# RWKV chunk loop on one core: token copies and two transposed inverses made two heads per product, heads laid out by parity of the pair

## What is computed

```python
def _wkv7_scan(r, decay, k, v, kk, a):          # 16 heads of 64
    def step(state, inp):
        r_t, w_t, k_t, v_t, kk_t, a_t = inp
        sk = jnp.einsum('bhij,bhj->bhi', state, kk_t)
        state = (state * w_t[:, :, None, :]
                 - sk[..., None] * (kk_t * a_t)[:, :, None, :]
                 + v_t[..., None] * k_t[:, :, None, :])
        y = jnp.einsum('bhij,bhj->bhi', state, r_t)
        return state, y
```

## Time and profile before

| what | value |
|---|---|
| median of 3 runs | 2909.34 us (2909.28 to 2913.61) |
| the profiled execution | 2909.81 us, its span 2907.8 us |
| busy in the span | PE 2583.3 us (89%), DVE 1611.4 (55%), POOL 1259.4 (43%), ACT 941.8 (32%) |
| first instruction of the recurrent stage on VectorE with data | 1628.8 us |
| first and last state update begin | 1700.6 and 2067.3 us |

### The profile page before, as it was taken

The page is one execution under the profiler, slowest core; times in us unless marked ns, Lnnn a source line. Parts: engine busy times, 40 slices in busy tenths (PEclk is TensorE's granted clock), DMA queues, the critical chain, the costliest instruction groups (busy, mean ns, idle before and its releaser), DMA issues. The chain is left out here.

```text
span 2907.8 us, 52077 instructions
## 1 busy us (share of the span) xinstructions
PE 2583.3 (89%) x21600; PEld 2089.2 (72%) x21600; DVE 1611.4 (55%) x1957; ACT 941.8 (32%) x1535; POOL 1259.4 (43%) x630
## 2 busy tenths in 40 slices
PE   2887888999999999989999577777799999999999
PEld 2565667788887788767777466666687888788887
DVE  7744455655543633376865489888335333434334
ACT  3435433322223222244544333333333222122221
POOL 3522334444445444444334345454355444444443
PEclk9889999999999999999999799989899999999999
DMA  7511224354442232237666544443332323232223
GB/s 254 186 61 38 87 88 152 130 181 160 168 144 89 86 106 96 94 98 188 156 176 159 123 102 105 98 98 71 102 126 75 107 94 99 84 104 99 96 100 123
DMA packets 299528, 342.01 MB, mean 118 GB/s; under 512 B 215072, under 2 KB 215200, under 8 KB 299296
## 3 DMA queue, kind: packets, MB, share of 16 engines
q1 hardware_dynamic: 299296, 338.69, 38.2%
HBM read 297.80 MB, written 39.85 MB: 116 GB/s over the span
## 5 line engine op out<-in xcount | busy, mean ns | idle before, releaser
L712 POOL TENSOR_TENSOR wl<-w,wh 128x1024 fp32r<-128x1024 f32 x367 | 904.0, 2470 | 1264.0 <-ACT wh L753 1264.0
L182 PE MATMUL ps<-hi,wh 128*128 128x512 f32 x2208 | 883.4, 400 | 25.6 <-ACT qk_raw L790 9.6
L183 PE MATMUL ps<-lo,wh 128*128 128x512 f32 x2208 | 869.8, 394 | 0.0
L184 PE MATMUL ps<-hi,wl 128*128 128x512 f32 x2208 | 869.5, 394 | 0.0
L753 ACT ACTIVATE wh<-w 128x1024 fp32r<-128x1024 f32 x367 | 387.0, 1056 | 681.6 <-DMA w<-in_ffn_w_in 522.2
L1025 DVE SCALAR_TENSOR_TENSOR xt<-ps,mod,xt 128x512 f32<-128x512 f32 x384 | 286.5, 750 | 420.7 <-PE ps L184 412.7
L182 PEld LDWEIGHTS ps<-hi,wh 128*128 128x128 f32 x2208 | 421.0, 191 | 129.0 <-issue 30.0
L183 PEld LDWEIGHTS ps<-lo,wh 128*128 128x128 f32 x2208 | 420.9, 191 | 90.0 <-issue 3.4
L184 PEld LDWEIGHTS ps<-hi,wl 128*128 128x128 f32 x2208 | 420.0, 190 | 90.0
L1030 DVE TENSOR_TENSOR act<-ps,silu 128x512 f32<-128x512 f32 x88 | 60.9, 692 | 477.9 <-PE ps L184 477.9
L182 PE MATMUL ps<-act_hi,wh 128*128 128x512 f32 x704 | 281.9, 400 | 17.3 <-DVE act_lo L1034 10.0
(11 more groups left out here) (225 smaller groups left out, 2891.0 us busy)
## 6 DMA issues: line engine op xcount, KB each, us to landing
w<-in_ffn_w_in SPq DMA_DIRECT2D x176, 512.0 KB, 3.4
piece<-in_ada_w SPq DMA_DIRECT2D x96, 512.0 KB, 4.6
w<-in_ffn_w_out SPq DMA_DIRECT2D x88, 512.0 KB, 3.4
w<-in_w_rkv SPq DMA_DIRECT2D x48, 512.0 KB, 4.0
scratch<-silu SPq DMA_DIRECT2D x48, 256.0 KB, 3.1
scratch<-act SPq DMA_DIRECT2D x48, 256.0 KB, 3.1
w<-in_wqk SPq DMA_DIRECT2D x20, 512.0 KB, 4.6
xt<-in_xT SPq DMA_DIRECT2D x4, 2048.0 KB, 11.0
```

The source lines that it names most:

```text
L182: pe.matmul(out, w_hi(k), x_hi(k), start=first and k == 0, stop=False)
L183: pe.matmul(out, w_hi(k), x_lo(k), start=False, stop=False)
L184: ins = pe.matmul(out, w_lo(k), x_hi(k), start=False, stop=last and k == kc - 1)
L712: pool.tensor_tensor(wl[n % NW][:, :, :], wr[n % NW][:, :, :], wh[n % NW][:, :, :].bitcast(F32), ALU.subtract).then_inc(*wlo.up)
```

## The change

It renames the layout. In the new `heads()` a head is (i, h, k): pair j = 2i + k, half h. Its own rows are half h, its token rows are now half k, the parity of the pair, and tiles are indexed by one of three slots. The two heads of neighbouring pairs with the same h then lie side by side in a 64 x 128 slice, so that one product with 128 weight columns copies both; `by_token` issues 8 products of 64x128 for 16 of 64x64. The transposed inverses of levels 0 and 1 are made in the same manner, as products of the finished inverse (ScalarE's copy) with `idst`; they wait for that copy (`t_done`) instead of the level's sum, and are issued in two halves k = 0 and k = 1 with a wait on `ut_half` between, since both halves write one PSUM bank. The last transposed inverse stays as it was. Waits on `ut_done` move from `level_sum` to `inverse_out`. And all five `period` lists are written anew: level 0 (`level_x`, `level_sum`, `level_inverse`) is done one period earlier in the pipeline, in the period of d; `squares`, `decay_up` and `decay_down` of ScalarE stand in the next period's list.

```diff
@@ by_token @@
-                            for j, hs, to in heads():
-                                ins = pe.matmul(spot(3, j, to), (vt_[ch % 2], bdec, kdec)[n][hs, j, :], idst[hs], start=True, stop=True)
+                            for i in range(QP):
+                                for h in range(2):
+                                    ins = pe.matmul(ps[:, 3 + h, i * CHUNK:(i + 1) * CHUNK],
+                                                    (vt_[ch % 2], bdec, kdec)[n][rows(h), 2 * i:2 * i + 2, :].rearrange("p a n -> p (a n)"), idst[rows(h)],
+                                                    start=True, stop=True)
@@ level_transposed @@
-                            pe.wait_ge(*g["w_done"].at(NL * ch + l + 1))
                             pe.wait_ge(*g["tt_done"].at(NL * ch + l))
-                            if l == 0:
-                                pe.wait_ge(*tt_in[ch % 2].at(4 * (ch // 2 + 1)))
-                            for j, hs, _ in heads():
-                                ins = pe.matmul(bank(2)[hs, j, :], wx[l % 2][hs, j, :], (tdiag_t[ch % 2], tinv_t, tdiag_t[ch % 2])[l][hs, j, :], start=True, stop=True)
+                            if l < NL - 1:
+                                pe.wait_ge(*g["t_done"].at(2 * ch + l + 1))
+                                for k in range(2):
+                                    if k == 1:
+                                        ins.then_inc(*g["ut_half"].up)
+                                        pe.wait_ge(*g["ut_half"].at(2 * ch + l + 1))
+                                    for i in range(QP):
+                                        ins = pe.matmul(bank(2)[:, k * QP + i, :], (tinv, tdiag[ch % 2])[l][rows(k), 2 * i:2 * i + 2, :].rearrange("p a n -> p (a n)"), idst[rows(k)],
+                                                        start=True, stop=True)
...
@@ SyncE period @@
-                            if d is not None:
-                                blocks_in(d)
-                            if w is not None:
-                                load_tiles(w)
...
+                                load_values(d)
+                            if zz is not None:
+                                transposed_back(zz)
+                            if d is not None:
+                                load_r(d)
+                            if zp is not None:
+                                load_gate(zp)
+                            if y is not None:
+                                blocks_out(y), blocks_in(y)
+                            if x is not None:
+                                load_tiles(x)
...
+                            if y is not None:
+                                inverse_out(y), transposed_out(y), inverse_back(y)
@@ GpSimd period @@
-                            if x is not None:
-                                keys(x)
                             if zq is not None:
                                 gate_values(zq)
                             if x is not None:
-                                normed_keys(x), gated_keys(x), bonus_terms(x)
+                                keys(x), normed_keys(x), gated_keys(x), bonus_terms(x)
@@ TensorE period (new list) @@
+                                by_feature(zp)
+                                by_token(x, 0)
                                 gram(d, 1)
+                                level_x(y, 1), level_transposed(y, 0)
                                 solve_u(zz)
+                                bonus_sums(x)
                                 outputs_and_state(zz)
+                                level_inverse(y, 1)
+                                gram(x, 0)
+                                level_transposed(y, 1)
+                                by_token(x, 1)
                                 level_x(y, 2)
                                 by_token(x, 2)
+                                level_x(d, 0)
+                                level_transposed(y, 2)
                                 norms(w)
+                                known_x(y)
+                                level_inverse(d, 0)
+                                solve_x(y)
@@ VectorE period (new list) @@
                                 bounded(x)
+                                scale(zp)
+                                level_masks(d)
                                 decayed_r(x)
+                                affine(zp)
                                 decayed_a(x)
+                                invert(d)
                                 level_sum(y, 1)
+                                products_k(d)
+                                decayed_b(x)
                                 transpose_blocks(d)
+                                decayed_keys(x)
                                 decay_sums(w)
+                                centre(zz), new_state(zz)
                                 scaled_keys(w)
+                                bonus_value(x)
+                                level_sum(y, 2)
                                 variance(zz)
+                                blocks_mask(x)
                                 key_gains(w)
+                                products_b(x)
+                                level_sum(d, 0)
```

More of the change, by code:

```diff
@@ L2 @@
 import math
+from collections import namedtuple
 from contextlib import ExitStack
@@ L1754, in known_x @@
                             pe.wait_ge(*g["yc_done"].at(ch))
-                            for j, to, hs in heads():
-                                ins = pe.matmul(spot(3, j, to), gk[b][hs, j, 0, :], vtok[ch % (RING + 1)][hs, j, :], start=j % QP == 0, stop=False)
+                            for n in heads():
+                                ins = pe.matmul(to_own(3, n), gk[b][n.token, n.t_slot, 0, :], vtok[ch % (RING + 1)][n.token, n.t_slot, :], start=n.i == 0, stop=False)
                             ins.then_inc(*g["x_known"].up)
@@ L1761, in solve_x @@
                             pe.wait_ge(*g["x_known"].at(ch + 1))
-                            for j, hs, _ in heads():
-                                ins = pe.matmul(spot(3, j, hs), ar[ch % (RING + 1)][hs, j, 0, :], state[hs, j, :], start=False, stop=j % QP == QP - 1)
+                            for n in heads():
+                                ins = pe.matmul(to_own(3, n), ar[ch % (RING + 1)][n.own, n.j, 0, :], state[n.own, n.o_slot, :], start=False, stop=n.i == QP - 1)
                             ins.then_inc(*g["xs_done"].up)
@@ L1770, in solve_u @@
                             pe.wait_ge(*g["xe_done"].at(ch + 1))
-                            for j, hs, to in heads():
-                                ins = pe.matmul(spot(3, j, to), inv[ch % 2][hs, j, :], xst[hs, j, :], start=True, stop=True)
+                            for n in heads():
+                                ins = pe.matmul(to_token(3, n), inv[ch % 2][n.own, n.o_slot, :], xst[n.own, n.o_slot, :], start=True, stop=True)
                             ins.then_inc(*g["us_done"].up)
@@ L1794, in outputs_and_state, with old_state @@
                             pe.wait_ge(*g["y_known"].at(ch + 1))
-                            for j, hs, _ in heads():
-                                if j >= QP:
-                                    ins = pe.matmul(spot(3, j, hs, HALF // 2), ar[ch % (RING + 1)][hs, j, 1, :], state[hs, j, :], start=False, stop=j % QP == QP - 1)
+                            for n in heads():
+                                if n.h != n.k:
+                                    ins = old_state(ch, n)
                             ins.then_inc(*g["chunk_used"].up)
+                        def old_state(ch, n):
+                            out, last = to_own(3, n, HALF // 2), n.i == QP - 1
+                            return pe.matmul(out, ar[ch % (RING + 1)][n.own, n.j, 1, :], state[n.own, n.o_slot, :], start=False, stop=last)
```

184 lines of the change are left out of this document (87 added, 97 removed).

## The result

The changed kernel takes 2934.12 us (median of 4 runs, 2926.22 to 2936.3), beside 2909.31 for the kernel before (4 runs, 2909.21 to 2913.61): ratio 1.008, 95% interval 1.0065 to 1.0094, slower by 0.8%. The forecast was 2898, with a range up to 2915. The profiled execution of the changed kernel took 2933.7 us, its span 2931.7: 23.9 us more than the span before.

| stage | before | after | difference | forecast |
|---|---|---|---|---|
| ahead of the loop (same code) | 1628.8 | 1634.8 | +6.0 | 0 |
| filling | 71.8 | 85.2 | +13.4 | +1 |
| 11 full periods | 287.9 | 280.7 | -7.2 | -11.7 |
| behind the full periods | 78.8 | 91.9 | +13.1 | 0 |
| rest | 840.5 | 839.2 | -1.3 | 0 |

The account below looks back on a forecast made before the run. It took VectorE's stream (24.1 us a full period) plus 2.05 us of waiting for TensorE as the bound. 2909.8 - 11.7 (full periods) + 0 (behind them) + 1 (filling) gave 2899, 2898 as median; range 2883 to 2915.

Parts of the forecast that it names:

- What bounds the kernel now: Full periods: 24.1 us of VectorE's own stream plus 2.05 waiting for TensorE, busy 212.7 of 287.8 us, no bound.
- (a): Token copies and inner transposed inverses, 16 products to 8: 2.4 us of TensorE instruction supply saved a period, array time unchanged.
- (c): Transposed inverses in two halves with a wait between: 1.4 us instead of 0.5, twice; +1.8 us of TensorE a period.
- (b): Changes of shape between wide groups and 64x64 groups: about 0.2 us each, 2.0 us of TensorE a period.
- (d): New order of VectorE's list: old waits covered; covers 1.1 (level 2), 1.6 (level 0), 1.0 (norms); 0.7 us waits a period.
- (e): VectorE instructions stalled by GpSimd products: 5.8 us a period against 5.4, so a stream of 24.4 us, bounds 23 and 25.5.
- (f): Block inverse's trip to memory and back within one period: hidden with 1 us to spare; transposed one back 24.1, wanted 24.5.
- The full periods: Loop's 11 full periods: 24.4 + 0.7 = 25.1 us each against 26.16, -11.7 us in all.
- The ends: Behind the full periods 0 (+7 wide groups, -4 records, -3 level 0 moved), bounds -5 and +6; filling +1.
- TensorE becomes the bound: Slower rival, chance 0.16: VectorE waits for a late TensorE stretch, period 27.4 us, +13 and +2 from drain, about 2925 us.

Follow-up runs that it names:

- order_only: Changed kernel with both wide forms undone, new order and layout kept: 2890.62 us, ratio 0.9944 to the kernel before; run again 2893.58 us, ratio 0.9957.
- copies_narrow: Changed kernel with the three token copies as 16 products of 64x64, transposed inverses still wide: 2896.77 us, ratio 0.9969 to the kernel before.

## Why the prediction was wrong, step by step

**What bounds the kernel now**: right, but one sentence of it misled. "TensorE is no bound by its work" rested on 212.75 busy of 287.8 us. Of the 75 us that it was idle, 51.7 were stops without a releaser, as in the earlier trace rows, time in which it could not have worked. Busy and starved together were 92% of the full periods; what was really free was 23 us, 2.1 a period.

**(a) the supply of instructions**: the mechanism was right. The stops fell from 51.7 us in the full periods to 5.6, 4.2 us a period where 2.4 was forecast. But it is no saving beside the next point: taken off the work, it assumes that the two add up, and by these figures the engine needs the longer of them. A period's 1,260 records (2 x 6929 / 11) are 4.9 blocks, 18.9 us at 3.85 each, already less than the 22.6 us of work. The same step said that "the array time of a copy stays". **This is the step that failed**: 1.04 us for 0.49, at the full clock, 1.90 at the lower. It counted rounds on the tiles and took a record of 128 weight columns to last as long as one of 64; the transposed inverse in (c) rests on the same count. Undoing the two wide forms took off 43 us (39.5 on one chip), more than the whole miss.

**(b) the changes of shape**: 0.1 rather than 0.2. Groups of like shape overlap by 0.17 us (1852.39 plus 1.10 against 1853.32 in TensorE's timeline of the changed kernel, with the earlier trace rows 0.20), a wide one and its neighbour by 0.07, so a change costs 0.1, inside the bounds (the ends of matmul records are modelled, so tenths are the most that can be read here). The rule that a change of mode drains the engine (the Trainium skill, TensorEngine Tiling (Array Packing), section Key Properties) would have the next group begin behind the end of the last; the trace does not show that between these groups, where the records still overlap by 0.07 us.

**(c) the transposed inverse**: 2.19 us for the 1.4 forecast, mostly the same error as in (a): the products take 1.53 and not 0.98, the wait 0.66 and not 0.4. The other side of the comparison was wrong as well: the group that it replaces was taken for one of 0.49 on four tiles, and took 0.93 on two; its row (1841.05, 1.07 us) is longer than that of the group ahead of it (0.69). With 0.1 for shapes, the five wide groups cost 3 x 1.14 + 2 x 2.29 = 8.0 us a period; the forecast had 3 x 0.89 + 2 x 1.8 = 6.3. At the full clock that is 1.7 us a period too little. Against the groups that they replace (3 x 0.49 + 2 x 0.93 = 3.3) TensorE got 4.7 us of work more a period, where (a) to (c) summed to 1.4.

**(d) the order and its cover**: the mechanism was right, the covers were too large. The waits of the earlier trace rows went, and those that came are in the three places named. But at the full clock the covers were 0.3 us for level 2 (the product over at 1794.89, wanted at 1795.20), 0.5 for level 0 and nothing for the norms, where 1.1, 1.6 and 1.0 were forecast. Two steps made them so large. Every group was placed as 0.49 us, while a wide copy takes 1.04 and a narrow group on two tiles 0.93. And the sum of level 0 was taken to need its own product alone (the 1.6 us between level 0 and the norms hold the transposed inverse, 0.5, and the norms, 1.1), while it also waits for that transposed inverse, 1.03 us more of TensorE. The changed kernel waited 20.8 us in eleven periods, 1.9 each, for 0.7 forecast within 0 to 3. With the narrow forms (order_only) it was 12.9 us, 1.2 each.

**(e) the stalls**: stream 23.6 us for the 24.4 forecast, within its bounds. b_dec takes 0.68, as forecast, the inversion 5.8 (1830.74 to 1836.52), but decayed_r 0.92 and not 1.7:

```profile
1828.22 0.92 DVE L1914 TENSOR_TENSOR ar<-r,e_pos 128x512 f32<-128x512 f32 x1
...
1830.74 1.28 DVE L2013 TENSOR_TENSOR t_diag<-n_diag,eye 128x64 f32<-128x64 f32 x1
...
1836.52 0.68 DVE L1977 TENSOR_TENSOR one_plus_x<-ps,con 128x512 f32<-128x512 f32 x1
1838.25 0.68 DVE L1928 TENSOR_TENSOR b_dec<-b,e_neg 128x512 f32<-128x512 f32 x1
```

**(f) the memory trips**: hidden in the changed kernel; no wait on them in its full periods. Where TensorE is faster they show a little: 2.0 us in order_only, 4.7 in copies_narrow, for the input of the inversion.

**The full periods**: -7.2 and -1.6 in the two profiled executions, for -11.7. At the full clock it would have been 11 x (23.6 - 26.17) = -28, an estimate. There the wide forms cost nothing that shows: order_only's periods at 1.00 took 23.1 to 24.8 us, the changed kernel's 23.4 to 23.8 in its two executions. So in the full periods the longer groups were paid for only where the clock had fallen and the covers were used up. The forecast priced every group at the full clock; only the rival on the slower side gave the norms 1 us for the lower one. In fact the lower clock lies on two copies, level groups and norms together, 10 us of a period at 0.81, and costs up to 3.7 us a period.

**The ends**: the largest error. Behind the full periods the forecast had +7 for the wide groups, -4 for supply, -3 for the level moved ahead. The last was right (order_only, -3.3). The supply was no saving for the reason in (a), the wide groups were priced too low as in (c), and the clock is 0.78 for 0.96, 40 us at the lower level where before had 6. There VectorE is busy 51 of 92 us and covers little, so wide groups stand in the chain; order_only, without them, took 75.5 us at 0.98. How much of the difference is array time and how much clock the runs do not separate. In filling the clock is 0.63 for 0.76, a transposed inverse takes over 3 us and a copy 1.90; +13.4 us, 10.3 of it gone in order_only. The forecast had looked for the memory trip there and put no TensorE work on the path.

**The rivals**: *TensorE becomes the bound* (0.16, about 2925) is what happened, with its place and nearly its size in the full periods of the worst sort (27.3 us; it said 27.4). It too had 2 us for the drain instead of 8 to 13, and nothing for filling. The forecast kept 0.60 against it because the wide groups were priced at 6.3 us a period and the covers at 1.0 to 1.6; with 8.0 and covers of 0 to 0.5 us the slower rival would have been the likelier.

**What stays open.** Why the clock falls more with the wide forms: the runs show that it does (0.90 and 0.87 against 0.97 and 0.98 in the full periods) and that undoing them brings it back, that in one period it fell some 2 us behind the wide inverse of level 1, with a single pause of 0.23 us (1840.55 to 1846.98 above), and also that in the first four periods the same instructions ran at 1.00. What decides between these was not found. Nor why the loop begins between 1623.4 and 1634.8 us in the profiled executions, whose code ahead of it is the same; the changed kernel had 1634.8 and 1629.9, order_only 1629.7 and 1624.4, so some 5 of the 40 us between them may lie there. Of the 24 us between the profiled executions of the changed kernel and of the one before, 6 do.

## What to carry to other kernels

Fewer and wider products are a gain only if the array's time per record stays; take it from a timed row of that very form, or measure it with a single group before rewriting the rest, and time the group that it replaces as well. Before trusting a cover, look up everything that the reader waits for, buffers included, and not only the product that it reads. Where an engine's idle time is starvation, removing records and adding work don't offset each other: compare the longer of the two with the period. And a loop with thin covers is to be summed at the lower clock too, and at its two ends, where no other engine's stream hides TensorE.

## What the runs showed of the hardware

- At the full clock a float32 group for 16 heads takes 0.49 us as 16 products on four 64x64 tiles, 0.93 as 16 on two of the four, 1.04 as 8 products with 128 weight columns alternating between the row halves, 1.53 with four on each half in turn, and 2.19 as the same with a wait of TensorE on itself between.
- A wide copy takes 0.89 us with 32 columns and 1.04 with 64: halving the columns saves 15%.
- A wait of TensorE on itself between two halves of a group costs 0.66 us with 128 weight columns and 0.1 to 0.3 with 64.
- The time of a full period stood near one of four values in 22 periods of two executions of the changed kernel, 23.6, 24.7, 26.3 and 27.3 us (none over 0.25 away), and each goes with one mean clock, 1.00, 0.93, 0.87 and 0.81.
